# Two small on-chip buffers made narrower, in a two-model transformer kernel

## The reference

```
mod = (silu(c) @ w_ada[l] + b_ada[l])          # 9 vectors of 1024 for a layer
h = rmsnorm(x, norm_g[l, 0]) * (1 + sc0) + sh0
x = x + 0.5 * g0 * (silu(h @ w_gate) * (h @ w_up)) @ w_down     # inner width 2816
x = x + g1 * token_mix(rmsnorm(x, ...) * (1 + sc1) + sh1)
x = x + 0.5 * g2 * ffn(rmsnorm(x, ...) * (1 + sc2) + sh2)
```

## Time and profile before

| | us |
|---|---|
| median of 3 runs | 4152.38 |
| lowest and highest of them | 4145.76, 4158.80 |
| the profiled execution's own time | 4152.38 |
| its span, first to last instruction | 4150.6 |
| PE busy | 3494.1 |
| DVE busy | 2200.8 |
| POOL busy | 1637.8 |
| ACT busy | 1233.5 |

### The profile page before, as it was taken

One profiled execution on the slowest core, in us unless ns is written; L12 is line 12 of the kernel. 1 busy time (PEld: TensorE's weight loads), 2 busy tenths in 40 slices (PEclk: granted clock), 3 DMA queues, 4 the chain that ended last, 5 costly groups with the idle time before them and its releaser, 6 DMA issues. The chain is left out here.

```text
span 4150.6 us, 44477 instructions
## 1 busy us (share of the span) xinstructions
PE 3494.1 (84%) x13472; PEld 2347.5 (57%) x13472; DVE 2200.8 (53%) x4476; ACT 1233.5 (30%) x2245; POOL 1637.8 (39%) x1127
## 2 busy tenths in 40 slices
PE   6999988899989999888999984795777776776877
PEld 4887745688878887456888762572333332332332
DVE  6536246433345452464333245286666666666766
ACT  3332215433233322154432225222222222222221
POOL 3446310244544464102445443124443443443542
PEclk9999987999999999979999996897898988987988
DMA  6535310122535353101234310118999999999997
GB/s 233 188 129 215 123 46 1 46 96 96 189 121 195 116 229 132 46 1 41 92 101 171 112 46 1 65 46 363 422 422 377 422 422 378 422 422 417 386 422 329
DMA packets 141092, 838.92 MB, mean 202 GB/s; under 512 B 15793, under 2 KB 16433, under 8 KB 63921
## 3 DMA queue, kind: packets, MB, share of 16 engines
q0 software_dynamic: 73728, 536.90, 31.1%
q1 hardware_dynamic: 67248, 300.56, 20.1%
HBM read 835.31 MB, written 2.10 MB: 202 GB/s over the span
## 5 line engine op out<-in xcount | busy, mean ns | idle before, releaser
L255 POOL TENSOR_TENSOR wlo<-wraw,whi 128x1024 fp32r<-128x1024 f32 x341 | 864.0, 2539 | 1360.8 <-ACT whi L251 1360.7
L2127 PE MATMUL g_psF<-g_ring,g_diagb 128*128 128x512 f32 x1792 | 853.9, 637 | 338.1 <-ACT g_diagb L2105 337.6
L2127 PEld LDWEIGHTS g_psF<-g_ring,g_diagb 128*128 128x128 f32 x1792 | 361.2, 205 | 833.1 <-issue 430.3
L2064 DVE CUSTOM_DVE_ANT_0 g_prod<-g_ring,g_xrow 128x1024 f32<-128x1024 f32 x448 | 548.8, 1225 | 174.8 <-DMA g_ring<-in_uv,g_ix 153.0
L251 ACT ACTIVATE whi<-wraw 128x1024 fp32r<-128x1024 f32 x341 | 361.0, 1059 | 810.9 <-DMA wraw<-in_wts 445.9
L262 PE MATMUL f_ps<-f_hh,whi 128*128 128x512 f32 x1408 | 552.2, 392 | 47.8 <-DVE f_hl L398 47.8
L2015 POOL DMA_INDIRECT g_ring<-in_uv,g_ix x448 | 470.4, 1050 | 206.0 <-issue 107.8
L263 PE MATMUL f_ps<-f_hl,whi 128*128 128x512 f32 x1408 | 551.1, 391 | 0.0
L264 PE MATMUL f_ps<-f_hh,wlo 128*128 128x512 f32 x1408 | 550.8, 391 | 0.0
L570 DVE TENSOR_TENSOR f_a<-f_sg,f_ps 128x512 f32<-128x512 f32 x88 | 60.5, 687 | 509.2 <-PE f_ps L264 487.2
L262 PEld LDWEIGHTS f_ps<-f_hh,whi 128*128 128x128 f32 x1408 | 266.5, 189 | 106.1 <-issue 51.0
(11 more groups left out here) (362 smaller groups left out, 5397.9 us busy)
## 6 DMA issues: line engine op xcount, KB each, us to landing
wraw<-in_wts SPq DMA_DIRECT2D x344, 512.0 KB, 3.5
m_wrow<-in_ada SPq DMA_DIRECT2D x52, 1024.0 KB, 6.9
m_erow<-in_ada SPq DMA_DIRECT2D x28, 1024.0 KB, 5.2
c_w<-in_w SPq DMA_DIRECT2D x2, 4096.0 KB, 12.1
wrawe<-in_wq SPq DMA_DIRECT2D x16, 512.0 KB, 3.5
g_ring<-in_uv,g_ix POOLq DMA_INDIRECT x448, 21.4
p_wt<-in_wtok SPq DMA_DIRECT2D x2, 3168.0 KB, 12.0
xT<-in_xT SPq DMA_DIRECT2D x1, 2048.0 KB, 12.1
```

Source lines behind the costliest of these rows:

```text
L255: self.nc.gpsimd.tensor_tensor(self.T.wlo[:, j % 4], self.T.wraw[:, j % 2], self.T.whi[:, j % 4].bitcast(F32), ALU.subtract).then_inc(self ...
L2064: nc.vector.tensor_tensor_reduce(prod[:, :], ub[s][k], xrow[:, :], 1.0, 0.0, ALU.mult, ALU.add, dot[:, s, k:k + 1]).then_inc(M["g_dot"], 1)
L2127: mm = nc.tensor.matmul(psF[:, c], diag[:, s, k], vb[s][k][:, c * S:(c + 1) * S], start=False, stop=False, skip_group_check=True)
```

## The change

Two widths are cut. Each column is 4 bytes in each partition, so `T.raw` goes from 448 to 320 bytes and `some` from 192 to 64 bytes.

```
@@ ffn
         lt = sb("f_lt", [P, 16])
-        some = sb("m_some", [P, 48])
+        some = sb("m_some", [P, 16])
@@ first_block
         T.gain = s1("gain", [P, 32])
-        T.raw = s1("raw", [P, 112])
+        T.raw = s1("raw", [P, 80])
         T.lam = s1("lam", [P, 16])
```

## The result

The changed kernel is slower: 4174.86 us (median of 7, 4172.32 to 4176.80) against 4151.49 us (median of 7, 4145.38 to 4159.88). The ratio is 1.0054, with a 95% interval of 1.0042 to 1.0066, or 23 us. The forecast was no change, 4138 to 4165 us, so the time lies outside the range.

The account below looks back on a forecast made before the run. It took PE to bound the first model, with DMA share 0.97 in the untouched PEER part; 4150.6 us of span, 0 added, and 1.8 us around it gave 4152.4 us, range 4138 to 4165 us.

Parts of the forecast that it names:

- The bound and the reach of the change: Only first-model tensors, 0 to 2345 us, shift, where PE is the bound outside the prologue; PEER stays at 1316 us.
- No instruction, no wait, no column missing: Whole kernel: no instruction or wait added, removed or moved, and the narrower widths still hold all columns used: 0 us.
- Matmuls whose operand moves: First model's 7488 matmuls with moved activation operands: 0 us taken; for 3264 at unseen places, bounds 10 and 46 us.
- The slower rival: Down projection and first model's two projections: PE reads activations worse at new places, up to 46 us, 4198 us; chance 0.08.
- the far bound: For the 3264 matmuls at unseen places: 14 ns each, between means of 389 and 403 ns, 46 us.
- the near bound: For the 3264 matmuls at unseen places: 3 ns each either way, 10 us.
- point of decision: Price per matmul from which the slower rival decides: 12.5 us over 3264 matmuls, 3.8 ns.
- DVE and ACT on moved tiles: Dot products and rounding take the same time at different places: 0 us taken, from 0 to 1 us either way.
- DMAs: Modulation-weight rows landing in moved tiles: 0 us taken, between -1.3 and +1.3; PE hides changes in the FFNs, nothing in the prologue.
- the rule of the Trainium skill: Prologue rows: transfers are cut at multiples of 256 bytes, so alignment would shorten the first 32 us by 0.5 us.
- The engines' moments: Rival: a small early difference changes which instructions meet, 4146 or 4159 us; its chance lies within no change's 0.80.

Follow-up runs that it names:

- `T.raw` alone: Against the kernel before, only `T.raw` made narrower (112 to 80 columns), `m_some` keeps 48: 4194.0 us, ratio 1.0101.
- the two with everything up: Kernel before with tiles 128 bytes later: from behind `T.eps` on, 4140.34 us; all but the compiler's constants, `xT` too, 4139.69 us.

## Why the prediction was wrong

**The bound and the reach of the change: right.** The first model alone changed, PE was its bound, and PEER kept its length within 1.5 us.

**No instruction, no wait, no column missing: right.** 13472 matmuls stand in both profiles, in the same order.

**Matmuls whose operand moves: this step failed.** It had two parts. For `f_hh` and `f_hl` both ends of the move were in the trace, and 0 was right: 227 ns before and after. For the other 3264 the step took 0 "as the medians are equal", and there 0 was wrong: 20.5 us. The working showed which places were unseen, and then argued from the seen ones. But 128 and 384 modulo 512, which I counted as two places, are the same place modulo 256, and the weights are at it too. So the "two places" that "give 389 ns as minimum and median alike" were one place seen twice, and equal medians over thousands of matmuls said nothing about the other. The experiment with everything up by 128 bytes shows that the quantity was the distance between operand and weights; the two with a half of the change show that 128 bytes of it cost and 256 don't.

**The rival that came true.** The slower rival had the right place (the down projection and the first model's two projections, 3264 matmuls) and the sign that would show it (393 ns or more, 231 ns from start to start; measured 392 to 395 and 232 to 234). Its price of 14 ns was the far bound, and 5.5 to 6.6 ns was measured, between the near bound of 3 ns and that one, above its point of decision at 3.8. It got a chance of 0.08, and the range ended at 13 us above, where the far bound alone would have taken it to 46. A bound that was worked out for an unseen place was then left out of the range because the seen ones were quiet.

**DVE and ACT on moved tiles: right.** The dot product stays at 1226 ns, and ACT's rounding is 722 ns into `f_hh` and into `p_hh`.

**DMAs: 0 in the sum, right; the cover held.** DVE's wait for the modulation rows was to "stay near 64 us" and fell to 39.4. It was no sign of anything: with the ring moved and nothing of the first model, it is 49.8 us. The last landing of the prologue came at 31.67 us instead of 31.99:

```profile
31.67 1.23 DVE L130 CUSTOM_DVE_ANT_0 m_prod<-m_wrow,crow 128x1024 f32<-128x1024 f32 x1 [3.00 <-DMA m_wrow<-in_ada]
```

That is 0.3 us earlier, and all twelve profiles together show that it is the place. From the start of the first dot product of the prologue to the start of this one it takes 24.71 to 24.82 us in the four whose `m0_wrow` starts at a multiple of 256 bytes (the changed kernel, `T.raw` alone, and the two with everything up), and 25.00 to 25.08 us in the eight where it doesn't. The prediction had 0.5 us by the rule of the Trainium skill (DMA: Bandwidth & Descriptors, How a descriptor splits into AXI transactions) and under 0.1 without it. The effect is there and is smaller than by that rule: 0.2 to 0.4 us of 25, 1.1%. In PEER, where DMA is full, it is 427 GB/s instead of 422 and a stage 1.1% shorter; an estimate from the rule's figures, 256 beats against 260, would make it 1.6%. The page tells the rule of what is read, while here the place that is written was what moved. I used this alignment on the prologue alone, where it was worth a third of a microsecond, while the ring of the stage that is bound by DMA stood unaligned in the same table of places, worth 15 us to anyone who moved it.

**The engines' moments:** no sign that they carry the result. The sum of spacings, with PEER's change where the ring moved, added to 4151 us, gives each run's time within 6 us; in these 6 us, and in the attention stages' scatter, they may have a part.

**A version that beats both kernels** is the kernel before with 128 bytes put in front of the ring: 4136.54 us, 0.9963 (0.9949 to 0.9977) of before.

## What to carry to other kernels

The size of a small tensor sets the address of everything behind it: where engines are full, note the starts of PE's moving operands and weights and of the tiles that DMAs fill, modulo 256, and keep the first two equal and the last at 0. Two measured places are evidence of a third only if they differ in the bit that the third one changes, and an unseen place keeps both its bounds in the range.

## What the runs showed of the hardware

- A 128x512 matmul on the fast float32 form, back to back at full granted clock, starts every 226.7 ns when operand and weights are equal modulo 256 bytes, and every 232 to 234 ns at distances of 32, 96, 128, 160, 192 and 224; 64 gives 228.9 (the distances other than 0 and 128 from one run, each on one kind of tile). The plain float32 matmuls of the same size (429 ns on `g_ring` and `g_diagb`, 128 and 64 modulo 256) don't change in any run.
- The cost isn't confined to the misplaced instruction: with one of three operands misplaced all three pay, and with one of two weight tiles misplaced two of three.
- Gathered rows of 8192 bytes land at 427 GB/s when their ring starts at a multiple of 256 bytes, and at 422 when it starts 64 or 128 bytes off. The 2 of 16 places that lie elsewhere go with the ring, whatever their own start.
- The prologue's rows of the modulation weight land over 24.7 to 24.8 us when their buffer starts at a multiple of 256 bytes, and over 25.0 to 25.1 us when it doesn't, in 4 and 8 profiles.
